# Rotated queries and keys turned in 32x32 blocks through memory, later modulation rows summed on VectorE, and three smaller moves of work in a two-layer trunk

## What is computed

```python
def pool_mixer(h, w_grp, ls):            # layer 0: windows 2, 4, 8, 16, 4 groups of 512 channels
    ... p = trailing mean - token; y = einsum(p, w_grp); return y * ls
def retention(h, w_in, w_out):           # layer 1: 8 heads, chunks of 128 tokens
    q, k, v, g = split(h @ w_in)         # 2048, 2048, 4096, 4096 columns
    q = rotary(q, pos); k = rotary(k, pos) * dk ** -0.5
    scores = einsum('bhid,bhjd->bhij', qc, kc) * intra
    inner = einsum('bhij,bhje->bhie', scores, vc); ...
    return (silu(g) * normed(y)) @ w_out
def sq_relu_mlp(h, w1, w2):
    a = relu(h @ w1); return (a * a) @ w2
def reference(x, c, ...):                # x (1, 256, 2048), 2 layers
    cond = silu(c)
    for i in range(2):
        mod = einsum('bd,sdk->bsk', cond, ada_w[i]) + ada_b[i]     # shift, scale, gate, twice
        h = modulate(rmsnorm(x, norm_g[i, 0]), shift_t, scale_t)
        x = x + gate_t * (pool_mixer if i == 0 else retention)(h)
        h = modulate(rmsnorm(x, norm_g[i, 1]), shift_m, scale_m)
        x = x + gate_m * sq_relu_mlp(h, mlp_w1[i], mlp_w2[i])
    return rmsnorm(x, final_g)
```

## Time and profile before

| | us |
|---|---|
| median of 3 runs | 2379.75 (2378.05 to 2380.79) |
| the profiled execution | 2379.09 |
| its span | 2377.3, granted clock 0.985 |
| TensorE busy | 2285.1 (96%) |
| VectorE busy | 1619.8 (68%) |
| ScalarE busy | 1088.6 (46%) |
| DMA engines | 272 GB/s over the span |

### The profile page before, as it was taken

How to read it: one execution, slowest core, us unless ns; L and a number is a source line. 1 busy time by engine, 2 the same in 40 slices (tenths; PEclk the granted TensorE clock), 3 DMA queues, 4 the chain that set the end, 5 groups by cost and what they waited for, 6 DMA issues and landing times.

```text
span 2377.3 us, 28744 instructions
## 1 busy us (share of the span) xinstructions
PE 2285.1 (96%) x10233; PEld 1836.9 (77%) x10233; DVE 1619.8 (68%) x1709; ACT 1088.6 (46%) x1352; POOL 88.9 (4%) x158
## 2 busy tenths in 40 slices
PE   4489999999999999999999999999999999999998
PEld 2147778888888887888888888887888888888887
DVE  4668887786886788667666767666876555555556
ACT  2324554544534545444444444455543453443454
POOL 0000010100100000000000000000100000000000
PEclk9689999999999999999999999999999999999999
DMA  9999899997988977766666766766897766766764
GB/s 401 415 412 397 307 338 328 359 338 267 370 306 282 354 268 248 246 223 221 222 224 227 248 212 222 232 219 210 326 341 244 232 214 195 225 209 195 228 202 155
DMA packets 270493, 645.50 MB, mean 272 GB/s; under 512 B 20385, under 2 KB 20721, under 8 KB 263313
## 3 DMA queue, kind: packets, MB, share of 16 engines
q1 hardware_dynamic: 260320, 611.92, 74.1%
q0 software_dynamic: 9136, 30.99, 3.7%
q10 hardware_dynamic: 896, 0.75, 0.1%
HBM read 628.87 MB, written 14.70 MB: 271 GB/s over the span
## 4 chain that ended last, share of the span: by engine, by line
PE 85%; DVE 3%; DMA 3%; ACT 1%; issue 1%; POOL 0%; POOLq 0%; DVEq 0%; ACTq 0%
PE acc L637 82%; DMA raw<-in_mlp_w 2%; DVE w_lo L1486 1%; PE tb L752 1%; PE acc L1033 1%; ACT w_hi L1088 1%; PE score_ps L1020 0%; DVE ada_acc L1492 0%; DMA scratch<-in_decay 0%; PE mod_ps L760 0%; PE tb L900 0%; PE score_ps L812 0%; DVE a_lo L2014 0%; DMA square_blocks<-ev 0%; DVE h_lo L1705 0%
## 5 line engine op out<-in xcount | busy, mean ns | idle before, releaser
L1486 DVE TENSOR_TENSOR w_lo<-raw,w_hi 128x1024 fp32r<-128x1024 f32 x775 | 945.7, 1224 | 655.7 <-ACT w_hi L1088 653.5
L1088 ACT ACTIVATE w_hi<-raw 128x1024 fp32r<-128x1024 f32 x775 | 821.3, 1060 | 1120.5 <-PE acc L637 1048.6
L637 PE MATMUL acc<-w_hi,h_lo 128*128 128x512 f32 x1788 | 700.1, 392 | 2.9 <-issue 2.2
L637 PE MATMUL acc<-w_hi,h_hi 128*128 128x512 f32 x1788 | 696.6, 390 | 0.0
L637 PE MATMUL acc<-w_lo,h_hi 128*128 128x512 f32 x1788 | 696.5, 390 | 0.0
L637 PE MATMUL acc<-w_hi,a_lo 128*128 128x512 f32 x1312 | 516.4, 394 | 5.0 <-DVE a_lo L2014 4.9
L637 PE MATMUL acc<-w_lo,a_hi 128*128 128x512 f32 x1312 | 513.0, 391 | 0.0
L637 PE MATMUL acc<-w_hi,a_hi 128*128 128x512 f32 x1312 | 512.8, 391 | 0.0
L637 PEld LDWEIGHTS acc<-w_hi,h_lo 128*128 128x128 f32 x1788 | 336.2, 188 | 75.1 <-issue 5.9
L637 PEld LDWEIGHTS acc<-w_hi,h_hi 128*128 128x128 f32 x1788 | 336.0, 188 | 70.1
L637 PEld LDWEIGHTS acc<-w_lo,h_hi 128*128 128x128 f32 x1788 | 336.2, 188 | 69.1
(11 more groups left out here) (183 smaller groups left out, 874.9 us busy)
## 6 DMA issues: line engine op xcount, KB each, us to landing
raw<-in_mlp_w SPq DMA_DIRECT2D x512, 512.0 KB, 4.6
ada_raw<-in_ada_w SPq DMA_DIRECT2D x248, 512.0 KB, 6.3
raw<-in_ret_w_in SPq DMA_DIRECT2D x192, 512.0 KB, 3.9
ada_early_h<-in_ada_w SPq DMA_DIRECT2D x32, 1024.0 KB, 13.3
raw<-in_ret_w_out SPq DMA_DIRECT2D x64, 512.0 KB, 4.3
ada_raw<-in_ada_w SPq DMA_DIRECT2D x16, 1024.0 KB, 12.5
square_blocks<-ev POOLq DMA_DIRECT2D x96, 128.0 KB, 5.1
ev<-square_blocks POOLq DMA_DIRECT2D x24, 512.0 KB, 6.0
```

The lines of the kernel that those rows point to most:

```text
L637: mm = nc.tensor.matmul(acc[pair][t][:], l[:, CK * c + j, tok], w[:, c % RING, j, :], start=first and j == 0 and i == 0, stop=last and j = ...
L1088: nc.scalar.activation(w_hi[:, o % RING], raw[:, o % RING], ACT.Copy).then_inc(hi_ready, 1)
L1486: nc.vector.tensor_tensor(w_lo[:, o % RING], raw[:, o % RING], w_hi[:, o % RING].bitcast(F32), ALU.subtract).then_inc(lo_ready, 1)
```

## The change

1. Rotated queries and keys are written in quarter order, turned in 32x32 blocks on VectorE (one instruction per q or k), and sorted through memory by GpSimd (four transfers out, one back). `scores` reads the queries as they come back; ScalarE puts the keys in order behind chunk 2 of unit 3 or 9, and the scores of a pair's first head move from behind chunk 1 to behind chunk 3 there. The TensorE transposes and the two ScalarE evacuations for each of q and k go.
2. The seven later modulation rows are summed on VectorE: turn 32x32 blocks of half the row's accumulator, reduce along the free axis, for both halves; four copies bring the quarters to one partition quarter, a reduce sums them; a gate is turned once more and added to its bias, a column is placed by four copies. TensorE's row sums and columns there go, and ScalarE's copy.
3. Group (0, 0) turns no squares through memory: all four units' squares are turned by TensorE (three more sets of eight transposes).
4. The halves of the turned squares are made in other places: unit 2 behind chunk 1 (behind chunk 5 in groups with half units), unit 3 behind chunk 1, unit 4 behind chunk 0.
5. The last `norm_fill` comes behind the column it stood before; the late rows' second part moves from behind chunk 3 of the seventh `p1` to behind chunk 0 of the eighth, and what follows it by a chunk.

```diff
+LOWER_AT = {0: (2, 1), 1: (3, 1), 2: (4, 0)}
+LOWER_AT_BEHIND_HALVES = {0: (2, 5), 1: (3, 1), 2: (4, 0)}
+def turns_of(layer, first):
+    return 0 if (layer, first) == (0, 0) else TURNED
-PE_STEPS = {1: {4: ["T rot"]}, 2: {3: ["T rot"]}, 3: {1: [("scores", 0)]}, 4: {3: [("weigh", 0)]},
+PE_STEPS = {3: {3: [("scores", 0)]}, 4: {3: [("weigh", 0)]},
-ACT_STEPS = {1: {4: [("q",)]}, 2: {3: [("k",)]}, 4: {3: [("y", 0)]}, 5: {1: [("z", 0)], 3: [("a", 0)]},
+ACT_STEPS = {3: {2: [("k",)]}, 4: {3: [("y", 0)]}, 5: {1: [("z", 0)], 3: [("a", 0)]},
...
+        rot_order = rot_blocks.rearrange("p (r t h two j) -> p t two h r j", r=4, t=TT, h=2, two=2)
+        qT = q_blocks.rearrange("p (q t k i) -> p k t q i", q=4, t=TT, k=4)
+        kT = scratch[:, 1024:2048].rearrange("p (k t) -> p k t", k=4)
...
-            for f in range(KT // 2):
+            for f in range(KT // 2 - 1):
                 norm_fill(f)
...
             column(score_ps)
+            norm_fill(KT // 2 - 1)
-            late_rows = {(4, 0): (0, 16), (6, 3): (16, SEG)}
+            late_rows = {(4, 0): (0, 16), (7, 0): (16, SEG)}
...
-                            if what == "gate" and u == 7:
-                                hooks[1] = [gate_row_sum]
-                            elif what and u == 7:
-                                hooks[1] = [row_sum]
-                                hooks[4] = [lambda: column(mod_ps)]
-                            if u == TURNED + 1:
+                            if turns_of(layer, first) < u <= 4:
...
             def scores(hd):
-                pe.wait_ge(tevac, n.of("TB"))
+                pe.wait_ge(rot_in, 2 * 16 * (n.n["SC"] // 2 + 1))
+                pe.wait_ge(k_ready, TT * (n.n["SC"] // 2 + 1))
...
+            def turn_row(h):
+                cols = slice(h * AW, (h + 1) * AW)
+                dve.wait_ge(ada_done, n.of("AD"))
+                nc.vector.transpose(ada_acc[:, cols], ada_acc[:, cols]).then_inc(row_turned, 1)
+                dve.wait_ge(row_turned, 2 * n.of("RT") + h + 1)
+                nc.vector.tensor_reduce(row_part[:, 32 * h:32 * h + 32], ada_acc[:, cols].rearrange("p (b i) -> p b i", i=32),
+                                        AX_X, ALU.add).then_inc(row_reduced, 1)
...
-                            if what == "gate" and u == 7:
-                                hooks[3] = [take_gate_row]
-                            elif what and u == 7:
-                                hooks[6] = [lambda: take_column(slice(r + 4, r + 5))]
+                            if what and u == 7:
+                                hooks = {0: [lambda: turn_row(0)], 1: [lambda: turn_row(1)],
+                                         2: [take_gate_row if what == "gate" else lambda: take_row(r + 4)]}
...
+                dve.wait_ge(rot_done, (n.of("RO") + 1) * TT)
+                nc.vector.transpose(rot_blocks, rot_blocks).then_inc(rot_turned, 1)
...
+            def turn_pair(pair):
+                for i, target in ((2 * pair, q_blocks), (2 * pair + 1, k_blocks)):
+                    pool.wait_ge(rot_turned, i + 1)
+                    for q in range(4):
+                        pool.dma_start(rotated[i % 2][:, :, q, :].rearrange("r j n -> j r n"),
+                                       rot_blocks[32 * q:32 * q + 32].rearrange("p (r n) -> p r n", r=4)).then_inc(rot_out, 16)
+                    pool.wait_ge(rot_out, 4 * 16 * (i + 1))
+                    if pair:
+                        pool.wait_ge(score_done, 2 * pair)
+                    if i:
+                        pool.wait_ge(rot_in, 16 * i)
+                    pool.dma_start(target, rotated[i % 2].rearrange("r j q n -> (r j) (q n)")).then_inc(rot_in, 16)
+
             for hd in range(HEADS):
+                if hd % 2 == 0:
+                    turn_pair(hd // 2)
```

More of the change, by code:

```diff
@@ L124, in spread_of, with lowered_in @@
     return ADA_SPREAD.get((layer, first), ADA_EVEN) if what else ADA_NONE
+def turns_of(layer, first):
+    return 0 if (layer, first) == (0, 0) else TURNED
+def lowered_in(layer, first, u):
+    at = LOWER_AT_BEHIND_HALVES if (layer, first) in HALVES else LOWER_AT
+    return [(w, at[w][1]) for w in range(turns_of(layer, first)) if at[w][0] == u]
 def part_of(layer, first, u):
@@ new lines, in take_row @@
+            def take_row(index):
+                total_row()
+                n.add(CS=1)
+                for r in range(4):
+                    placed = nc.vector.tensor_copy(mod_col[32 * r:32 * r + 32, index, :],
+                                                   row_sums.rearrange("p (k r) -> p r k", r=4)[:, r, :])
+                placed.then_inc(row_placed, 1)
+                dve.wait_ge(row_placed, n.of("CS") - 4)
+                nc.vector.tensor_tensor(mod_col[:, index, :], mod_col[:, index, :], bias_col[:, index, :],
+                                        ALU.add).then_inc(col_used, 1)
@@ L2048, in group @@
                             n.add(SB=3)
-                        if what == "col":
-                            n.add(RM=1)
                     if trips == 1:
```

208 lines of the change are left out of this document (114 added, 94 removed), and 2 rows, old and new, of the table ACT_STEPS.

## The result

The changed kernel takes **2358.24 us** (median of 4 runs, 2357.60 to 2359.25) beside 2379.11 (2378.05 to 2380.79) of the kernel before on the same chip: ratio 0.9913, interval 0.9901 to 0.9925, 20.9 us less. The forecast was 2360, range 2353 to 2371. The profiled execution took 2358.18, its span 2356.4. In a later set of runs the same kernel took 2359.33, ratio 0.9909 (0.9892 to 0.9925).

What follows compares the result with a forecast made beforehand. The prediction took TensorE as the bound: the end moves by what it executes plus what it idles. Its terms summed to -19.7 us, from 2379.75 to 2360 us, range 2353 to 2371.

Steps and rivals of the forecast that it cites:

- stall at the first rotation: Retention's first round: query rotation waits for the decay table, so VectorE's turn there is late in full, +1.3 us.
- The whole boundary hangs on it: +4.5: Last unit of group (0, 3): VectorE's row sum brings the boundary's first step 3.3 us later; with the row's 1.24, +4.5.
- Retention's last unit, +2.1: Unit before the next norm: TensorE idles 0.5 and 1.5 us for VectorE's weights, +2.1 us.
- One chunk later the sum is ready.: Late rows' last sum of the fifth early part: moved one chunk, its 2.59 us wait and slow matmuls go, -4.2 us.
- A full 128x128 turn is eight transposes.: Rotated queries and keys: a turn takes eight transposes and two evacuations, 0.87 us of TensorE, against 1.24 on VectorE.
- VectorE becomes the bound: Rival at the row sums: a slow reduce makes a unit's extra work pass VectorE's spare, 2380 to 2395 us, 4%.
- The idle times in the last units drop the clock: Rival in the units before a norm: idle times lower the clock, 1.6 us each, 2362 to 2364 us, 15%.
- Strided queries: Rival in the score matmuls: queries in pieces of 32 columns read at half speed, 2372 us, 7%.
- keys late: Rival in retention: contention doubles the transfers' landings, four pairs wait 1 to 3 us each, 2364 to 2372 us, 6%.
- The turn is not hidden: Rival in retention: VectorE's 1.24 us turn shows behind all eight rotations, 2369 us, 6%.
- The start is bound by DMA: Rival in the start: DMA, not TensorE, bounds it, so gains come back as waits for weights, 2364 to 2368 us, 10%.
- point 5: Late rows moved one chunk later, -4.2 us, and the last `norm_fill` moved behind the column, nothing.

Runs made afterwards that it cites:

- experiment 1: The changed kernel with the rotated queries and keys turned on TensorE again, the rest kept: 2364.87 us, ratio 0.9936.
- experiment 2: The changed kernel with the row sums and columns behind 400 us on TensorE again, the rest kept: 2362.37 us, ratio 0.9929.
- experiment 3: The changed kernel with the squares of group (0, 0) turned through memory again, the rest kept: 2362.01 us, ratio 0.9921.
- experiment 12: The changed kernel with first half row and other groups' sums earlier, decay table counted apart, gate's total later, and group (0, 0) through memory again: 2353.52 us.
- experiment 4: The changed kernel with the halves of the turned squares back behind chunk 2 in every group, the rest kept: 2362.20 us, ratio 0.9927.
- experiment 5: The changed kernel with the late rows' sum, the column behind it and the norm's last fill at their places of before: 2363.73 us, ratio 0.9933.
- experiment 9: The changed kernel run once more, code unchanged: 2359.33 us, ratio 0.9909.
- experiment 6: The changed kernel with each 1024-element reduce on VectorE done twice, nothing else changed: 2368.96 us, ratio 0.9955.
- experiments 8: The changed kernel with the decay table counted apart, so the first rotation waits only for cosines and sines: 2357.38 us, ratio 0.9906.

## Why the prediction was right

The mechanism was the one forecast: the end moves by TensorE's executed time plus its idle time. The path in the two units before a norm was not (below). Each term of the sum, with what the runs put in its place:

| term | forecast | measured | by |
|---|---|---|---|
| eight sets of transposes | -7.0 | -7.2 | experiment 1 (8 x 0.9) |
| stall at the first rotation | +1.3 | +1.6 | experiment 1; 1.3 in both traces |
| row sums, the five units with room | -7.5 | -7.6 | experiment 2 |
| last unit of (0, 3), row less idle | +3.3 | +2.6 | experiment 2, both traces |
| retention's last unit, the same | +0.4 | +1.3 | experiment 2, both traces |
| group (0, 0) | -1.9 | -2.1 | both traces; 0 and -2.6 in experiments 3, 12 |
| halves | -4.1 | -4.0 | experiment 4 |
| late row and last fill | -4.2 and 0 | -4.3 | experiment 5; -4.2 in both traces |
| sum | -19.7 | -19.7 | |

Of the 20.9 between the two spans 1.2 are left. 0.8 lie before the first `p1`, in the part that DMA bounds; experiment 1 had a start 1.8 later than the kernel after with the same code there, so nothing is concluded from it. Another 0.4 lie between two groups of layer 1, where the two kernels do the same.

Steps that were wrong or mis-sized:

- **"The whole boundary hangs on it: +4.5"** (last unit of (0, 3)). The boundary's first step did come 3.3 us later against its unit, exactly as walked, but only 2.6 of it reached retention's first product, because the path is another: from the unit's last matmul to that product it is 3.18 us before and 3.19 after. What costs are TensorE's two waits. By the starts each costs its idle time and 0.27 us more: around the idle time of 1.89, from 886.73 to 889.34, two steps take 2.61 us in place of 0.45, 2.16 more. That gives 1.89 + 1.31 + 0.54 = 3.7, less the row sum's 1.24, 2.5.
- **Retention's last unit, +2.1.** The same account gives 0.69 + 1.75 + 0.54 = 3.0, less 1.67, which is the 1.3 measured. The waits are 0.4 longer than the 2.0 forecast, and the 0.5 behind them was left out. One reason is in the trace: the row's total takes 2.26 us (1630.48 to 1632.74) where at most 1.9 was taken, 0.60 of it for the small reduce that was put among operations of 0.15 to 0.4.
- These two errors, -0.7 and +0.9, cancel. That the sum is right to 0.1 us is luck to that extent.
- **"One chunk later the sum is ready."** It is not; TensorE still waits 1.41 us for it. The products ahead of it run 2.4 us earlier than before (0.8 from the start, 1.6 from eight slow matmuls from 189.49 on, which the prediction did not look for), and the sum comes only 0.7 earlier. That what is won ahead of the sum is waited for in front of it is the prediction's own clause on the last fill ("then waits that us: nothing"), and so the -4.2 for the two came out.
- **The stall at the first rotation, +1.3.** It is 1.3 between the two traces, but TensorE's wait there, 1.50 us in the kernel after, is 0.94 in experiment 9 with the same code and 2.48 in experiment 3. The agreement is that of one pair of executions.
- **"A full 128x128 turn is eight transposes."** A set of eight turns eight blocks of 128x128. The prices, 0.87 against 1.24 for the same data, are right all the same.

The rivals. "VectorE becomes the bound" was priced with the right mechanism: with another 1.2 us per reduce (experiment 6) the kernel loses 10.7 us. By the trace the two units before a norm pay at once. In the other five the spare of the last `w_lo` is 1.2, 2.4, 2.4, 2.9 and 3.7 us of VectorE's time in the kernel after, and in experiment 6 the first of them pays. What it left out is the clock: 24 matmuls run slow there, 0.2 us each, 4.8 in all. The point from which the sign turns was not reached: at 2.4 us per reduce half of the gain is still there, and more was not tried. "The idle times in the last units drop the clock" occurs in three of the seven kernels with those idle times, at 2.3, 2.3 and 0.3 us where 1.6 was given; 15% looks too low, though the result's own profile doesn't show it. "Strided queries" and "keys late" show in no trace. "The turn is not hidden" is true at the first rotation only, but by 0.2 us in the closest of the others. "The start is bound by DMA" is true as to the sum's arrival, and yet point 5 kept its 4.2 us.

The rule of the Trainium skill (VectorE: DVE Perf Modes, Rules for kernel authors), by which a 128x128 turn that may go to PSUM belongs on TensorE, would not have let the change win the 7.0. Here the measurement decides against it: 0.9 us of TensorE per set of eight, against 1.245 of VectorE and a trip through memory that cost nothing in seven of eight places. By the Trainium skill (VectorE: DVE Perf Modes, The perf-mode tier table) `tensor_reduce` gains no speed; that agrees with the trace: 1220 ns for 1024 elements, the 1223 of the two-input `lo`.

## What to carry to other kernels

When one engine is busy for 96% of the span, moving its small work to an engine with idle time pays in full where that engine's own slack, counted in chunks before use, is larger than the work; look for the units where chunks are shorter or where the helper already does a boundary's work, for there it costs more than it brings, and try the same work one unit earlier. Taking away a short wait of the bound engine may be worth more than its length, since matmuls behind it can run at half the clock: price each wait with the matmuls that follow it in the trace. And time won ahead of something that comes at its own time, a sum bound by the arrival of weights here, is only waited for there. An undone part shows its worth at its place in the trace to 0.1 us, where medians of four runs scatter by one or two.

## What was not expected of the hardware

- The same waits of TensorE in the last unit of (0, 3) (2.25 and 1.71 us between starts) brought 7 to 12 matmuls at the lower level in three kernels and none in four others with the same work there. After 2.52 us of idle time in experiment 3 none ran at the lower level; after 3.43 in experiment 12, eight. In experiments 8 and 9 eight did behind waits that the kernel after has without them.
- Copies on 32 partitions take 182 ns for 64 elements and 165 ns for 16: small steps have a floor that a sum by elements misses. A reduce of 256 elements to 64 on 32 partitions takes 605 ns, half of what one of 1024 to 32 on 128 takes (1220); why is open.
- Queries that matmuls read in 256 columns of 32-column pieces cost as much as contiguous ones: the group's mean is 327 ns in both kernels.
- A wait of TensorE costs 0.27 us more than its idle time in the profile, by the starts of the matmuls around it: 2.16 us for 1.89, 2.02 for 1.75 and 0.96 for 0.69.
